# GpSimd makes the first keys' weighted one-hot matrices, between its row fetches

## The reference

```python
def block(hb):
    q = (hb @ w_q).reshape(n, PEER_HEADS, 2, PEER_HALF)
    s = jnp.einsum('nhid,hikd->nhik', q, sub_keys).astype(jnp.float32)
    s_top, i_top = lax.top_k(s, PEER_TOPK)
    cand = s_top[:, :, 0, :, None] + s_top[:, :, 1, None, :]
    cand_idx = i_top[:, :, 0, :, None] * PEER_N_KEYS + i_top[:, :, 1, None, :]
    best, pos = lax.top_k(cand.reshape(n, PEER_HEADS, PEER_TOPK * PEER_TOPK), PEER_TOPK)
    idx = jnp.take_along_axis(cand_idx.reshape(n, PEER_HEADS, -1), pos, axis=-1)
    w = jax.nn.softmax(best, axis=-1)
    u = jnp.take(u_tab, idx, axis=0)
    act = jax.nn.gelu(jnp.einsum('nhkd,nd->nhk', u, hb).astype(jnp.float32))
    out = jnp.einsum('nhk,nhkd->nd', w * act, jnp.take(v_tab, idx, axis=0))
```

## Time and profile before

| | us |
|---|---|
| median of 3 runs | 3185.7 (3184.34 to 3189.09) |
| the profiled execution | 3184.96 |
| its span, first to last instruction | 3183.2 |
| PE busy | 3064.9 (96%) |
| PE weight loads busy | 2804.8 (88%) |
| VectorE busy | 2172.2 (68%) |
| ScalarE busy | 1153.5 (36%) |
| GpSimd busy | 407.1 (13%) |

### The profile page before, as it was taken

The page is one execution under the profiler, slowest core; times in us unless marked ns, Lnnn a source line. Parts: engine busy times, 40 slices in busy tenths (PEclk is TensorE's granted clock), DMA queues, the critical chain, the costliest instruction groups (busy, mean ns, idle before and its releaser), DMA issues.

```text
span 3183.2 us, 43033 instructions
## 1 busy us (share of the span) xinstructions
PE 3064.9 (96%) x17723; PEld 2804.8 (88%) x17723; DVE 2172.2 (68%) x3782; ACT 1153.5 (36%) x1569; POOL 407.1 (13%) x264
## 2 busy tenths in 40 slices
PE   7999998999999999999999999999999979999998
PEld 7888887878879888998877879999999979999998
DVE  6436875755743443577763468897997758999897
ACT  2224233222233341555553222444445523333332
POOL 0000000000000000000000000010111145665552
PEclk9889998999999998999999999999999989999999
DMA  6233113222232133212124333547777799999996
GB/s 233 88 114 146 40 43 117 76 87 103 75 137 80 64 108 135 80 67 80 67 100 166 119 119 124 197 165 232 258 239 247 273 351 392 403 403 402 401 401 247
DMA packets 215714, 571.10 MB, mean 179 GB/s; under 512 B 14288, under 2 KB 129488, under 8 KB 180064
## 3 DMA queue, kind: packets, MB, share of 16 engines
q1 hardware_dynamic: 176496, 426.14, 37.2%
q0 software_dynamic: 36864, 134.23, 11.2%
q10 hardware_dynamic: 2160, 7.99, 0.6%
HBM read 495.95 MB, written 72.35 MB: 179 GB/s over the span
## 4 chain that ended last, share of the span: by engine, by line
PE 75%; DVE 14%; DMA 6%; ACT 3%; issue 1%; SPq 1%; DVEq 0%; ACTq 0%
PE bank L578 67%; DMA wv<-weight_spill 4%; DVE wl L533 3%; PE bank L1241 2%; DVE acc L149 2%; PE bank L642 2%; DMA gelu_spill<-gst 1%; PE bank L2512 1%; PE bank L590 1%; PE bank L649 1%; DVE Ah L3047 1%; PE bank L2521 1%; ACT wh L526 1%; PE bank L1506 0%; SPq L3056 0%
## 5 line engine op out<-in xcount | busy, mean ns | idle before, releaser
L578 PE MATMUL bank<-hh,wh 128*128 128x512 f32 (+2 forms) x2512 | 920.4, 366 | 31.7 <-DVE wl L533 15.4
L578 PE MATMUL bank<-hl,wh 128*128 128x512 f32 (+2 forms) x2512 | 895.3, 356 | 0.0
L578 PE MATMUL bank<-hh,wl 128*128 128x512 f32 (+2 forms) x2512 | 890.6, 355 | 0.0
L533 DVE TENSOR_TENSOR wl<-ring,wh 128x2048 fp32r<-128x2048 f32 (+2 forms) x249 | 554.4, 2226 | 306.8 <-ACT wh L526 306.2
L526 ACT ACTIVATE wh<-ring 128x2048 fp32r<-128x2048 f32 (+2 forms) x249 | 463.7, 1862 | 783.0 <-PE bank L578 774.2
L578 PEld LDWEIGHTS bank<-hh,wh 128*128 128x128 f32 x2512 | 481.7, 192 | 87.2 <-issue 18.1
L578 PEld LDWEIGHTS bank<-hl,wh 128*128 128x128 f32 x2512 | 481.7, 192 | 49.7 <-issue 6.0
L578 PEld LDWEIGHTS bank<-hh,wl 128*128 128x128 f32 x2512 | 481.6, 192 | 45.7
L3243 POOL DMA_INDIRECT ub<-in_urow,gsel x128 | 193.8, 1514 | 1448.0 <-DVE gsel L2974 875.9
L578 PE MATMUL bank<-ph,wh 128*128 128x384 f32 x1024 | 347.2, 339 | 9.6 <-DVE pl L3206 6.7
L578 PE MATMUL bank<-ph,wl 128*128 128x384 f32 x1024 | 345.8, 338 | 0.0
(11 more groups left out here) (519 smaller groups left out, 4423.0 us busy)
## 6 DMA issues: line engine op xcount, KB each, us to landing
ring<-in_v SPq DMA_DIRECT2D x68, 1024.0 KB, 17.6
ring<-in_u SPq DMA_DIRECT2D x64, 1024.0 KB, 5.6
ring<-in_ada SPq DMA_DIRECT2D x24, 1024.0 KB, 4.9
gelu_spill<-gst SPq DMA_DIRECT2D x128, 192.0 KB, 3.5
weight_spill<-stage SPq DMA_DIRECT2D x24, 1024.0 KB, 8.2
gv<-gelu_spill SPq DMA_DIRECT2D x64, 384.0 KB, 11.2
wv<-weight_spill SPq DMA_DIRECT2D x64, 384.0 KB, 15.3
ring<-in_wup SPq DMA_DIRECT2D x22, 1024.0 KB, 4.8
```

Source lines behind the costliest of these rows:

```text
L533: v.then_inc(v.e.tensor_tensor(wl[q % 2][:, 0:n], ring[k % 4][:, 0:n], wh[q % 2][:, 0:n].bitcast(F32), S_), s("parts"))
L578: ins = p.e.matmul(out, l, r, start=start and i == 0, stop=stop and i == len(pairs) - 1, skip_group_check=not check)
```

## The change

In blocks 1 to 3 the weighted first-key matrices `Ah` are made by GpSimd, with the same four operations a quad, and counted by a semaphore `ah` of their own; VectorE makes `Bh` alone, counted by `ab`. PE waits for both. GpSimd's list is no longer the row fetches alone, but its own weave by the same `choose`: `hot_po` (five idle steps, then the quads) with `rows_po`, which at the step where VectorE works on row n fetches row n+2. The first two rows are fetched at the start of `top(1)`. From row 48 on the fetches are as before, behind all of that.

```diff
@@ hot_pe
             p.wait_ge(s("ab"), t + 1)
+            p.wait_ge(s("ah"), t + 1)
@@ hot_ve
         if j >= 2:
             v.wait_ge(s("ab"), 32 * j - 32)
+            v.wait_ge(s("ah"), 32 * j - 32)
         v.then_inc(v.e.tensor_copy(ijw, bank[4][:, 0:384].rearrange("p (c k) -> p c k", c=3)), s("ijw"))
         v.settle()
         for t, q in quads(j):
             if t >= 2:
                 v.wait_ge(s("ab_mm"), t - 1)
-            v.e.tensor_tensor(Bh[t % 2][:, :, :], rep(C["iota"], 4), bc(ijw[:, 1, 4 * q:4 * q + 4], 128), ALU.is_equal)
+            v.then_inc(v.e.tensor_tensor(Bh[t % 2][:, :, :], rep(C["iota"], 4), bc(ijw[:, 1, 4 * q:4 * q + 4], 128),
+                                         ALU.is_equal), s("ab"))
+            yield
+        for _ in range(3):
+            yield
+
+    def hot_po(g, j):
+        for _ in range(5):
+            yield
+        g.wait_ge(s("ijw"), j)
+        for t, q in quads(j):
+            if t >= 2:
+                g.wait_ge(s("ab_mm"), t - 1)
             for z in range(4):
                 k = 4 * q + z
-                ins = v.e.tensor_scalar(Ah[t % 2][:, z, :], C["iota"], ijw[:, 0, k:k + 1], ijw[:, 2, k:k + 1],
-                                        ALU.is_equal, M)
-            v.then_inc(ins, s("ab"))
-            yield
-        for _ in range(3):
-            yield
+                ins = ts(g.e, Ah[t % 2][:, z, :], C["iota"], ijw[:, 0, k:k + 1], ALU.is_equal, ijw[:, 2, k:k + 1], M)
+            g.then_inc(ins, s("ah"))
+            yield
+        yield
@@ in place of gather_po
+    def fetch_row(g, n):
+        if n == 0:
+            g.wait_ge(s("gsel"), 2)
+        if n == RT:
+            g.wait_ge(s("wst0"), WST[0])
+        if n < RT and n >= 2:
+            g.wait_ge(s("gd"), n - 1)
+        elif n >= RT + 4:
+            g.wait_ge(s("gd"), n - 5)
+        b = ub_of(n)
+        g.e.indirect_dma_start(ub[b][:, :], None, D["urow" if n < 128 else "vrow"],
+                               bass.IndirectOffsetOnAxis(gsel[:, 0, n % 128:n % 128 + 1], 0)
+                               ).then_inc(s(f"ub{b}").sem, 16)
+
+    def top_po(g, j):
+        if j == 1:
+            for n in range(2):
+                fetch_row(g, n)
+        yield from top_idle(j)
+
+    def rows_po(g, n0, n1):
+        for n in range(n0 + 2, n1 + 2):
+            if n < RT:
+                fetch_row(g, n)
+            yield
+
+    def choose_po(g):
+        yield from choose(turn_idle(), lambda j: top_po(g, j), lambda j: hot_po(g, j), lambda m, n: rows_po(g, m, n),
+                          start_idle())
+
+    def experts_po(g):
+        run(choose_po(g))
+        for n in range(RT, 256):
+            fetch_row(g, n)
@@ pool
         gprep_po(g)
-        gather_po(g)
+        experts_po(g)
```

More of the change, by code:

```diff
@@ L3043, in hot_ve @@
                 v.wait_ge(s("ab_mm"), t - 1)
-            v.e.tensor_tensor(Bh[t % 2][:, :, :], rep(C["iota"], 4), bc(ijw[:, 1, 4 * q:4 * q + 4], 128), ALU.is_equal)
-            for z in range(4):
-                k = 4 * q + z
-                ins = v.e.tensor_scalar(Ah[t % 2][:, z, :], C["iota"], ijw[:, 0, k:k + 1], ijw[:, 2, k:k + 1],
-                                        ALU.is_equal, M)
-            v.then_inc(ins, s("ab"))
+            v.then_inc(v.e.tensor_tensor(Bh[t % 2][:, :, :], rep(C["iota"], 4), bc(ijw[:, 1, 4 * q:4 * q + 4], 128),
+                                         ALU.is_equal), s("ab"))
             yield
@@ L3052, in hot_ve @@
             yield
+    def hot_po(g, j):
[5 more added lines that the diff above has]
+                g.wait_ge(s("ab_mm"), t - 1)
+            for z in range(4):
+                k = 4 * q + z
+                ins = ts(g.e, Ah[t % 2][:, z, :], C["iota"], ijw[:, 0, k:k + 1], ALU.is_equal, ijw[:, 2, k:k + 1], M)
+            g.then_inc(ins, s("ah"))
+            yield
+        yield
     def spill(y, b, z):
```

## The result

The changed kernel takes 3437.9 us (median of 4 runs, 3434.3 to 3445.5) against 3187.4 us in the same comparison: ratio 1.0796, 95% interval 1.0781 to 1.0811. It is 250 us slower. The sign was forecast, but 3437.9 lies above the range's end of 3415, and the loss is 1.8 times the 140 us of the sum.

What follows compares the result with a forecast made beforehand. PE was taken to bound the kernel, busy 96% of the span. Stalls 125, old idle -13, other stalls 6 and clock 22 made +140 us on 3185: 3325 us, range 3250 to 3415.

Steps and rivals of the forecast that it cites:

- the sum: Over the stage: stalls 125 (36 P - 33.6), old idle -13, other stalls 6, clock 22: +140 us.
- The chain: Between quads T-1 and T: VectorE `Bh` of T+1, row, GpSimd fetch, four `Ah`; stalls PE at 36 places, 125 us.
- The hand-over P: From a row's end to PE's start: 4.0 us plus 0.4 port trouble, 4.4 us; bounds 3.3 and 6.2.
- Stalls away from fetches: At adjacent quads and the two starts of a weave: +6 us, an estimate.
- The clock: Slower PE clock after some 20 of 36 stalls, 2.9 us or longer: 22 us, bounds 0 and 60.
- the -13: Old PE waits in the stage (8.3 us) and the slower clock after them go: 13 us back.
- A: In the stage, VectorE's relief shows and the chain doesn't bind: faster, 3172 us; 4%.
- B: Most row ends far enough ahead; only some 25 us of stalls beside the 13 given back: near 3190 us; 4%.
- C: The chain binds at the cheap hand-over, 3.3 us, with hardly any clock loss: +72, 3257 us; 20%.
- D: The forecast: hand-over P from 3.8 to 5.4 us with some clock loss, 3290 to 3385 us; 50%.
- E: GpSimd and VectorE shut each other out at the SBUF port in nearly every quad: P 6.2, 3408 us; 22%.
- The signs that were named: Stage: 36+ `Ah` waits, 3 to 4 us, behind fetches; against: waits not following fetches, or VectorE's waits for PE vanishing.

Runs made afterwards that it cites:

- experiment 2: Changed kernel, five idle steps kept, each row below 48 fetched one row step later so the fetch's wait is already met: 3253.8 us, 1.022.
- experiment 1: Changed kernel with three idle steps, not five, ahead of GpSimd's quads, so GpSimd stands two quads ahead of PE: 3245.5 us, 1.019.
- experiment 6: Changed kernel plus 717 useless matmuls on PE before its `ah` wait, fitted to the wait at each of 38 quads: 3390.5 us, 1.0643.
- experiment 7: Changed kernel, five idle steps and early fetches kept, two of each quad's four `Ah` back on VectorE: 3366.6 us, 1.057.
- experiment 3: Changed kernel's GpSimd order and waits, but VectorE makes all four `Ah` and GpSimd does one single-column operation instead: 3334.0 us, 1.046.
- experiment 8: As experiment 1, but VectorE makes all four `Ah` in the last block: 3194.9 us, 1.0034.
- experiment 4: As experiment 1, but each quad's four `Ah` divided, two on VectorE and two on GpSimd: 3184.1 us, 0.9995.
- experiment 9: As experiment 4, but the last block's `Ah` all on VectorE: 3180.2 us, 0.9986.
- experiment 10: As experiment 9, but one of four `Ah` on GpSimd in place of two in the first two blocks: 3178.2 us, 0.9993.

## Why the prediction was right in kind and wrong in size

**The chain: right.** All its links are in the trace, 38 waits stand behind a fetch where 36 or more were forecast, and they go when the fetch's wait goes (experiment 2) or when the quad is ahead of it (experiment 1). Place by place the sum holds. For quad 10 it gives 7.4 (VectorE) + 4.6 - 4.1 (two half tiles) = 7.9 us, measured 8.4. For quad 3 it gives 5.2 + 6.4 - 4.1 = 7.5, measured 7.62.

**The hand-over P: mis-sized.** I took 4.4 us. It was 4.5 to 4.6 us in 27 of the 38 places, 6.4 us in ten and 7.4 us in one; in these eleven `wl` met it. The mean is 5.15. With it the formula gives 36 x 5.15 - 33.6 = 152 us, and 168.4 less the three starts of blocks (4.28, 4.27 and 4.17 us) is 155.7, 31 more than the 125 forecast. The miss lies in one price: an `Ah` alone takes 0.78 us, not 0.5.

```profile
L145 POOL TENSOR_SCALAR Ah<-cst,hl_u x384: 780/782/3592, 2059.9 to 2784.8; 128x128 f32<-128x128 f32 x192
```

My bounds were 0.32 and 0.86; I chose by the row of the same engine, and the truth lay near the other end. Four of them are 1.1 us more in each hand-over. The fetch (1.03 us where I had 1.32) and the step from it to `Ah` (2123.02 to 2123.06, where I had 0.3) gave 0.55 of it back, and the meetings with `wl` took 0.5 on average for my 0.4 of port trouble: P was short by 0.7 to 0.8, 27 of the 31 us.

**Stalls away from fetches: too small.** +6 was forecast. The three starts are 12.7 us and the 11 other waits 17.4: 30.

**The clock: the largest miss.** I took 22 us of a bound of 60, and 5 us of old clock were to go with the -13, so 17 net; the busy time rose by 78. The step that failed has two parts. The first is the count: I took 20 stalls of 2.9 us or longer, and there were 31, since the hand-overs were longer than forecast and the starts of blocks joined them. They are the right ones to count: 31 of the 35 stretches at the lower clock stand at one of them, and only four at shorter waits alone. My price of each was right too: 31 at 1.7 to 3.0 us are 53 to 93 us, and 78 + 5 were measured. The second part is the discount: I let waits hide more than half. In the changed kernel each of the 31 stretches began between 3.5 us before the end of its wait and 1.0 us behind it, and most of the lower clock fell on useful work: PE worked in 148 of its 195 us. Experiment 6 bears it out with its 47 us. Over the runs the extra busy time goes with the waits for `Ah`: 78 us for 186, 60 for 135 (experiment 7, busy 3125.0), 47 for 113 (experiment 3, 3111.7), 19 for 55 (experiment 2, 3084.1), 18 for 50 (experiment 1, 3083.2), and none for 18 or 8 (experiments 8 and 4). So here a microsecond of frequent stall cost 1.4.

Together: 31 + 24 + 61 = 116 us, less the 5 that overlapping ends hide: 111, and the gap between 140 and 250 is 110.

**Rivals.** A and B were out, as said. C's cheap price was wrong. D, the forecast, held in mechanism, and its P of up to 5.4 held on average (5.15); its clock did not. E, that GpSimd and VectorE shut each other out in nearly every quad, is half right. No run shows a port as the cause: not of E's P of 6.2, not of my 0.4, and not where an expectation names it. What the runs show is a GpSimd operation that begins within a pass of VectorE and outlasts it:

```profile
2196.03 2.57 DVE L533 TENSOR_TENSOR wl<-ring,wh 128x2048 fp32r<-128x2048 f32 x1 [0.66 <-ACT wh L526]
```

```profile
2196.71 2.56 POOL L145 TENSOR_SCALAR Ah<-cst,hl_u 128x128 f32<-128x128 f32 x1
```

Here an `Ah` that otherwise takes 0.78 us ended at 2199.27, 0.67 us behind the end of `wl`. Eleven `Ah` of the changed kernel began within a pass of `wl`: ten ended 0.66 or 0.67 us behind its end, one 1.72 us. But `wl` met eleven of 38 hand-overs, not nearly all, since GpSimd mostly worked while VectorE stood waiting for PE; P was 5.15 us on average, and 6.4 or more in those eleven alone.

**The signs that were named.** Waits follow fetches, and VectorE's waits for PE in the stage grew (to 329.8 us) and did not vanish, so neither sign against the chain came. Less exact were the sizes: the waits behind fetches were 4.4 us on average, not 3 to 4, and `Ah` was 0.78 us alone and 0.94 on average, not 0.4 to 0.7. One reading was too narrow: the fetches of before that met no `wl` took up to 1.39 us, not 1.15.

**That nothing is given back behind the stage** was right (646.5 and 646.0 us). VectorE's relief was worth no more than was said: experiments 4, 9 and 10 leave PE 5 to 8 us of waits for `Ah` and gain 0 to 4 us.

## What to carry to other kernels

When an engine's list gets a second kind of work, ask of each wait in it what is queued behind it, and who wants that next: here a harmless wait for a buffer, put in front of work two steps from its use, cost more (149 us with next to no work behind it) than the work itself (61 us, given a lead). Give the engine the same lead in program order as the engine that it takes the work from, or put the transfer where its condition is already met. And where PE is the pace, price a stall above its length: here the clock behind 186 us of waits made the matmuls 78 us dearer.

## What the runs showed of the hardware

A tensor_scalar with two per-partition scalars took GpSimd 0.78 us for 128 columns (the median of 384 in the changed kernel); one with a constant took 0.20 to 0.24 us for a single column (experiment 3, where it stands alone). VectorE needed 0.26 us for the same 128 columns, four in a row.

The mean of such a time can mislead, since GpSimd's operations took longer beside VectorE's. The single column has a mean of 0.435 us, of 0.22 alone and 2.3 beside `wl`. The mean of the same `Ah` was 0.94 us in the changed kernel, 1.16 in experiment 1 and 1.33 in experiment 4, the more of them met VectorE's passes. VectorE lost little: the median pass of `wl` took 2.29 us before, after and in experiment 1, the longest 2.51, 2.57 and 2.52 us.

And 717 useless calls in the stalls made the changed kernel 47 us faster (experiment 6).
